# Feed-forward tail: modulation and residual folded into the accumulated rows ahead of the last products, sum of squares on ScalarE

## The reference, cut to what matters

```
def conv_glu(h, w_ffn_in, conv_w, conv_b, w_ffn_out):
    gate, val = jnp.split(h @ w_ffn_in, 2, axis=-1)            # D_FF = 2816 each
    gconv = conv_b + sum(gp[:, j:j + T] * conv_w[j] for j in range(CONV_W))
    return (jax.nn.gelu(gconv) * val) @ w_ffn_out

    x = x + gt1 * (mix @ lw['w_out'])                          # kept as x1
    h2 = rmsnorm(x, lw['g_ffn']) * (1.0 + sc2) + sh2
    x = x + gt2 * conv_glu(h2, ...)                            # gt2: a row of 1024, one per group
    ...
    y_prompt = rmsnorm(x_ctx, g_final)
    y_sample = rmsnorm(x_lat, g_final)
```

## Time and profile before

| what | value |
|---|---|
| runs | 2257.80, 2255.67, 2257.38 us; median 2257.38 us |
| profiled execution, its own time | 2254.62 us |
| its span, first to last instruction | 2252.8 us |
| mean granted TensorE clock | 0.971 |
| TensorE matmul busy | 2118.3 us (94%) |
| VectorE, ScalarE, GpSimd busy | 964.6 us (43%), 670.3 us (30%), 782.2 us (35%) |

### The profile page before, as it was taken

How to read it: one execution, slowest core, us unless ns; L and a number is a source line. 1 busy time by engine, 2 the same in 40 slices (tenths; PEclk the granted TensorE clock), 3 DMA queues, 4 the chain that set the end, 5 groups by cost and what they waited for, 6 DMA issues and landing times. The chain is left out here.

```text
span 2252.8 us, 28053 instructions
## 1 busy us (share of the span) xinstructions
PE 2118.3 (94%) x11544; PEld 1949.0 (87%) x11544; DVE 964.6 (43%) x1372; ACT 670.3 (30%) x954; POOL 782.2 (35%) x512
## 2 busy tenths in 40 slices
PE   7499999999999988999988789999999999999995
PEld 2489999999999977788878777999999999999994
DVE  2613434444313126556624438343344333433348
ACT  1334232323213242677753211311211121112120
POOL 0324252526113414445532522422332233223234
PEclk9699999999999989999999899999999999999998
DMA  6366111112121356233345331311111111111113
GB/s 236 112 214 83 38 52 31 53 31 66 59 72 44 96 149 180 62 95 105 93 112 153 129 120 66 94 47 38 47 39 47 38 48 47 38 38 47 48 66 131
DMA packets 189103, 183.88 MB, mean 82 GB/s; under 512 B 52743, under 2 KB 156896, under 8 KB 188976
## 3 DMA queue, kind: packets, MB, share of 16 engines
q1 hardware_dynamic: 187680, 177.37, 26.5%
q0 software_dynamic: 1296, 4.72, 0.6%
HBM read 141.32 MB, written 40.74 MB: 81 GB/s over the span
## 5 line engine op out<-in xcount | busy, mean ns | idle before, releaser
L129 POOL TENSOR_TENSOR s_w_lo<-s_w_raw,s_w_hi 128x1024 fp32r<-128x1024 f32 x86 | 219.9, 2558 | 509.0 <-ACT s_w_hi L124 509.0
L822 PE MATMUL s_psum<-h_hi,s_w_hi 128*128 128x384 f32 x1008 | 345.3, 346 | 26.1 <-POOL h_lo L250 26.1
L2525 PE MATMUL s_ps<-h_hi,s_w_hi 128*128 128x384 f32 x1056 | 353.3, 335 | 0.7 <-ACT gate_pad L2368 0.7
L2525 PE MATMUL s_ps<-h_hi,s_w_lo 128*128 128x384 f32 x1056 | 353.1, 334 | 0.0
L2525 PE MATMUL s_ps<-h_lo,s_w_hi 128*128 128x384 f32 x1056 | 353.1, 334 | 0.0
L822 PE MATMUL s_psum<-h_hi,s_w_lo 128*128 128x384 f32 x1008 | 337.9, 338 | 0.0
L822 PE MATMUL s_psum<-h_lo,s_w_hi 128*128 128x384 f32 x1008 | 337.9, 338 | 0.0
L822 PEld LDWEIGHTS s_psum<-h_hi,s_w_hi 128*128 128x128 f32 x1008 | 191.1, 190 | 36.1 <-issue 19.0
L2525 PEld LDWEIGHTS s_ps<-h_hi,s_w_hi 128*128 128x128 f32 x1056 | 198.3, 188 | 1.4 <-issue 1.0
L2525 PEld LDWEIGHTS s_ps<-h_lo,s_w_hi 128*128 128x128 f32 x1056 | 198.3, 188 | 0.4
L2525 PEld LDWEIGHTS s_ps<-h_hi,s_w_lo 128*128 128x128 f32 x1056 | 198.3, 188 | 0.0
(11 more groups left out here) (366 smaller groups left out, 3877.4 us busy)
## 6 DMA issues: line engine op xcount, KB each, us to landing
s_w_raw<-in_w_ffn_in SPq DMA_DIRECT2D x44, 512.0 KB, 3.7
s_w_raw<-in_w_in SPq DMA_DIRECT2D x41, 512.0 KB, 3.9
s_w_mod<-in_w_mod SPq DMA_DIRECT2D x8, 2048.0 KB, 8.0
w_raw<-in_w_ffn_out SPq DMA_DIRECT2D x11, 1024.0 KB
scratch_gates<-sig SPq DMA_DIRECT2D x48, 192.0 KB, 1.9
merge_gates<-scratch_gates SPq DMA_DIRECT2D x16, 576.0 KB, 4.4
w_mod<-in_w_mod SPq DMA_DIRECT2D x4, 2048.0 KB, 10.1
scratch_o_mla<-o_raw SPq DMA_DIRECT2D x8, 576.0 KB, 4.8
```

Of the source, the lines that this page charges most:

```text
L129: pool.tensor_tensor(flat[0], flat[1], flat[2], ALU.subtract).then_inc(self.lo_ready, 1)
L822: return pe.matmul(bank(j), wx[c % 2][:, k, :], hx[:, k, j * CH:(j + 1) * CH], start=(k == 0 and n == 0), stop=(k == KD - 1 and n == 2))
L2525: mm = pe.matmul(ps[bank][:, 0:CH], a[s][:, k, :], b[:, k, j * CH:(j + 1) * CH], start=n == 0, stop=n == 3 * KD - 1)
```

## The change

It does five things. (1) Ahead of the last products DVE multiplies each `yacc` tile by the `gt2` row (`z_gate`) and POOL adds the residual half by half (`z_add`), in the order tile 8 (the context), then 0 to 7. `z_gate(0)` stands in pair 9 after `y_add(8)`, `z_gate(1)` to `(4)` after the values of pair 9, `(5)` to `(8)` between the two convolutions of pair 10. On POOL `z_add(0)` and `(1)` stand ahead of `split_lo(42)`, `(2)` to `(4)` ahead of `split_lo(43)`, `(5)` and `(6)` ahead of `u_split(10, 0)`, `(7)` and `(8)` after `u_split(10, 1)`. (2) In the tail DVE multiplies the PSUM halves by the `gt2` row straight into `x2`, and POOL adds the `yacc` tile (DVE does it for the last tile). (3) The sum of squares is taken by ACT with an accumulating Square. (4) The residual is loaded in halves into a ring of four, the first four in pair 9 with a `gt2` row (`gt2_once`, loaded twice), the other 14 each after the `z_add` four halves before. (5) The convolution buffers start at a lower address. PE's stream is the same but for the semaphore of L2618.

```
         late = Arena(nc, after_h)
         yacc = late("yacc", [P, TILES, D])
-        over = Arena(nc, home.top)
+        over = Arena(nc, first.at)
...
+        gt2_once = over("gt2_once", [P, D])
+        x1_back = [over("x1_back3", [P, HALF])]
...
+        x1_back = [late(f"x1_back{i}", [P, HALF]) for i in range(3)] + x1_back
...
+        Z_TILES = (TILES - 1,) + tuple(range(TILES - 1))
...
+                def load_back(i):
+                    t, half = Z_TILES[i // 2], i % 2
+                    if i >= 4:
+                        sp.wait_ge(z_ready, i - 3)
+                    sp.dma_start(x1_back[i % 4][:, :], io["x1"][t * P:(t + 1) * P, half * HALF:(half + 1) * HALF]
+                                 ).then_inc(back_loaded[i % 4], 16)
...
                 for g in range(PAIRS):
+                    if g == LAST - 1:
+                        sp.dma_start(gt2_once[:, :], io["rows"][3:4, :].to_broadcast([P, D])).then_inc(once_loaded, 16)
+                        for i in range(4):
+                            load_back(i)
                     if g < LAST:
                         load_win(4 * g + 4)
                         load_win(4 * g + 5)
                         load_w2(g + 1)
+                    if g == LAST - 1:
+                        sp.wait_ge(z_gated, 1)
+                        sp.dma_start(gt2_once[:, :], io["rows"][2:3, :].to_broadcast([P, D])).then_inc(once_loaded, 16)
+                    if g < LAST:
                         load_win(4 * g + 6)
                         load_win(4 * g + 7)
+                for i in range(4, O_UNITS):
+                    load_back(i)
                 sp.wait_ge(v_ps, 6 * PAIRS)
...
                 for t in range(TILES):
-                    if t >= 3:
-                        sp.wait_ge(e_x2, t - 2)
-                    sp.dma_start(x1_back[t % 3][:, :], io["x1"][t * P:(t + 1) * P, :]).then_inc(back_loaded[t % 3], 16)
...
                     sp.wait_ge(e_fin, t + 1)
...
                 for t in range(TILES):
+                    act.wait_ge(e_x2, t + 1)
+                    if t >= 3:
+                        act.wait_ge(e_stored[t % 3], 16 * (t // 3))
+                    act.activation(fin[t % 3][:, :], x2[t % 3][:, :], ACT.Square, accum_out=stat[:, 3, t:t + 1]).then_inc(e_sq, 1)
                     act.wait_ge(e_sq, t + 1)
...
+                def z_add(n):
+                    pool.wait_ge(z_gated, n + 1)
+                    for i in (2 * n, 2 * n + 1):
+                        cols = slice(i % 2 * HALF, (i % 2 + 1) * HALF)
+                        pool.wait_ge(back_loaded[i % 4], 16 * (i // 4 + 1))
+                        z = yacc[:, Z_TILES[n], cols]
+                        pool.tensor_tensor(z, z, x1_back[i % 4][:, :], ALU.add).then_inc(z_ready, 1)
...
+                z_add(0)
+                z_add(1)
+                w.split_lo(pool, 0, 4 * LAST + 2)
+                for t in range(2, 5):
+                    z_add(t)
+                w.split_lo(pool, 1, 4 * LAST + 3)
+                z_add(5)
+                z_add(6)
+                u_split(LAST, 0)
+                w2_split(LAST)
+                u_split(LAST, 1)
+                z_add(7)
+                z_add(8)
+
+                pool.wait_ge(z_ready, O_UNITS)
+                for t in range(TILES - 1):
+                    pool.wait_ge(e_gated, 2 * t + 2)
+                    pool.tensor_tensor(x2[t % 3][:, :], x2[t % 3][:, :], yacc[:, t, :], ALU.add).then_inc(e_x2, 1)
...
-                        pe.wait_ge(e_sum, o - 7)
+                        pe.wait_ge(e_gated, o - 7)
...
+                def z_gate(n):
+                    t = Z_TILES[n]
+                    dve.wait_ge(once_loaded, 32 if n else 16)
+                    if n == 0:
+                        dve.wait_ge(y_added, O_UNITS * Y_PAIRS)
+                    dve.tensor_tensor(yacc[:, t, :], yacc[:, t, :], gt2_once[:, :], ALU.mult).then_inc(z_gated, 1)
+
                 for g in range(PAIRS):
                     conv_gate(g, 0)
                     if 0 < g < LAST:
                         y_add(g - 1)
+                    if g == LAST - 1:
+                        z_gate(0)
+                    if g == LAST:
+                        for n in range(5, TILES):
+                            z_gate(n)
                     conv_gate(g, 1)
                     value(g, 0)
                     value(g, 1)
...
+                    if g == LAST - 1:
+                        for n in range(1, 5):
+                            z_gate(n)
...
+                def end_gate(t):
+                    if t >= 3:
+                        dve.wait_ge(e_fin, t - 2)
                     for half in range(2):
                         o = 2 * t + half
+                        cols = slice(half * HALF, (half + 1) * HALF)
                         dve.wait_ge(e_ps, o + 1)
...
+                        dve.tensor_tensor(x2[t % 3][:, cols], ps[(6 + o) % 8][:, :], gt2[group(t)][:, cols], ALU.mult).then_inc(e_gated, 1)
...
                 for t in range(TILES):
-                    end_sums(t)
+                    end_gate(t)
+                    if t == TILES - 1:
+                        dve.wait_ge(e_gated, 2 * TILES)
+                        dve.wait_ge(z_ready, O_UNITS)
+                        dve.wait_ge(e_x2, TILES - 1)
+                        dve.tensor_tensor(x2[t % 3][:, :], x2[t % 3][:, :], yacc[:, t, :], ALU.add).then_inc(e_x2, 1)
                     if t >= 1:
-                        end_square(t - 1)
                         end_scale(t - 1)
-                end_square(TILES - 1)
                 end_scale(TILES - 1)
```

More of the change, by code:

```diff
@@ L2216, in stage_out_ffn @@
         w2_raw = over("w2_raw", [P, 2, D])
-        assert over.at <= HIGH
+        gt2_once = over("gt2_once", [P, D])
+        x1_back = [over("x1_back3", [P, HALF])]
+        assert over.at <= HIGH - 8
         w2_hi, w2_lo = late("w2_hi", [P, 2, D], F32R), late("w2_lo", [P, 2, D], F32R)
         u_hi, u_lo = late("u_hi", [P, 2, NT], F32R), late("u_lo", [P, 2, NT], F32R)
+        x1_back = [late(f"x1_back{i}", [P, HALF]) for i in range(3)] + x1_back
         assert late.at <= first_end
@@ L2235, in stage_out_ffn @@
         gfin = end("g_final_row", [P, D])
-        x1_back = [end(f"x1_back{i}", [P, D]) for i in range(3)]
         x2 = [end(f"x2_{i}", [P, D]) for i in range(3)]
@@ L2253, in stage_out_ffn @@
         y_ps, y_added = sems("y_product"), sems("y_added")
-        end_rows, back_loaded = sems("end_rows"), [sems(f"back_loaded{i}") for i in range(3)]
-        e_ps, e_sum, e_gated, e_x2 = sems("end_product"), sems("end_sum"), sems("end_gated"), sems("end_x2")
+        end_rows, once_loaded, back_loaded = sems("end_rows"), sems("once_loaded"), [sems(f"back_loaded{i}") for i in range(4)]
+        z_gated, z_ready = sems("z_gated"), sems("z_ready")
+        e_ps, e_gated, e_x2 = sems("end_product"), sems("end_gated"), sems("end_x2")
         e_sq, e_std, e_rstd = sems("end_sq"), sems("end_std"), sems("end_rstd")
@@ L2319, in _ @@
                     sp.dma_start(gt2[g][:, :], io["rows"][2 + g:3 + g, :].to_broadcast([P, D])).then_inc(end_rows, 16)
+                g_final = io["g_final"]
+                sp.dma_start(gfin[:, :], bass.AP(g_final.tensor, g_final.offset, [[0, P], [1, D]])).then_inc(end_rows, 16)
                 for t in range(TILES):
-                    if t >= 3:
-                        sp.wait_ge(e_x2, t - 2)
-                    sp.dma_start(x1_back[t % 3][:, :], io["x1"][t * P:(t + 1) * P, :]).then_inc(back_loaded[t % 3], 16)
[L2324 to L2331, removed]
                     sp.wait_ge(e_fin, t + 1)
@@ L2478, in _ @@
                 w.split_lo(pool, 0, 2)
-                for g in range(PAIRS):
+                def z_add(n):
[5 more added lines that the diff above has]
+                        pool.tensor_tensor(z, z, x1_back[i % 4][:, :], ALU.add).then_inc(z_ready, 1)
+                for g in range(LAST):
                     if g > 0:
@@ L2482, in _ @@
                     w.split_lo(pool, 1, 4 * g + 3)
-                    if g < LAST:
-                        w2_split(g)
+                    w2_split(g)
                     u_split(g, 0)
[L2486 to L2489, removed]
+                    w.split_lo(pool, 0, 4 * g + 4)
                     u_split(g, 1)
[L2491 to L2497, removed]
+                    w.split_lo(pool, 1, 4 * g + 5)
+                z_add(0)
[15 more added lines that the diff above has]
+                    pool.tensor_tensor(x2[t % 3][:, :], x2[t % 3][:, :], yacc[:, t, :], ALU.add).then_inc(e_x2, 1)
             @block.tensor
@@ L2721, in _ @@
                     value(g, 1)
-                def end_sums(t):
+                    if g == LAST - 1:
+                        for n in range(1, 5):
+                            z_gate(n)
+                dve.wait_ge(end_rows, 48)
+                def end_gate(t):
+                    if t >= 3:
+                        dve.wait_ge(e_fin, t - 2)
```

(8 more changed lines are left out.)

## The result

The first four runs of the changed kernel gave a median of 2237.19 us against 2256.98 before: ratio 0.9914, interval 0.9897 to 0.9931. That is faster, as forecast, but 0.8 under the low end of the range. With more runs on one chip (six against eleven) it was 2238.74 against 2256.38, ratio 0.9926, interval 0.9914 to 0.9938.

A forecast was written before the change was run, and what follows sets the result against it. VectorE was taken to bound the tail, 6.88 us a tile against TensorE's 5.53. The rearranged tail gave 15.8 less, TensorE's wait in pair 10 took back 1.0; 14.8 off the median 2257.38 gives 2242.6, range 2238 to 2249.

The forecast's parts named there:

- the sign that VectorE would wait for TensorE in every tile: Tail: VectorE's tile at 4.4 us, under TensorE's 5.53, so VectorE waits in every tile.
- That chain: Last tile, TensorE's end 2227.72 to scaling's end 2232.8: half product, add, square, root, reciprocal, scaling.
- The unseen price: Last tile's square on ScalarE: handing out the sum, between 0 and 0.3 us, taken as 0.1.
- Pair 10's locked work: VectorE and POOL in turn, from 2140.8 to the last convolution step: 24.7 us, so to 2165.5.
- the term of 1.0 for TensorE's wait in pair 10: Second value chunk in pair 10: TensorE waits 0.6 us, raised to 1.0 for lock turns and a late load.
- The store term of 0.3: Span's end: last two stores 1.6 us apart instead of 3, between 0 and 1.8 more, taken as 0.3.
- the 216 matmuls: Tail products: TensorE needs 49.8 us for all of them, 5.53 a tile.
- the low end: Whole time 2238: no wait (1.0 less), no store crowding (0.3), runs as low as the profiled one (2.8 below median).
- Rival 1: Pair 10: TensorE waits longer, from full locked work or a late half load, 4 to 10 us; around 2250, chance 0.12.
- Rival 2: Tail: a table load of 1.28 us between Square and root, perhaps doubled; 2244 to 2245, chance 0.08.
- Rival 3: Tail: VectorE or the lock still sets the pace, tile near 6.9 us; time near 2257, chance 0.04.
- Rival 4: Pair 10: late half loads hold POOL's in-order queue, TensorE stands 18 us or more; 2262 to 2270, chance 0.04.

The follow-up runs named there:

- experiments 2 and 3: Kernel before with only the sum of squares moved to ScalarE, ratio 0.9963; changed kernel with that sum back on VectorE, ratio 0.9955.
- no_z: Changed kernel without the moved gate multiplications, residual adds and their loads; from pair 10's first product to the span's end 133.2 us.
- after_again: Changed kernel run again without an edit; ratio 0.9926, from pair 10's first product to the span's end 133.35 us.
- extra1: Changed kernel plus one VectorE operation of 1,024 columns before pair 10's second convolution; from pair 10's first product to the span's end 137.1 us.
- extra2: Changed kernel plus two VectorE operations of 1,024 columns before pair 10's second convolution; from pair 10's first product to the span's end 140.3 us.

## Why the prediction was right and wrong

**Right, and shown.** The mechanism is the forecast's. TensorE never waited for VectorE before, and VectorE's tile of 6.9 against TensorE's 5.5 made the tail; with the tile under 5.5 the end is one tile's chain behind TensorE (experiments 2 and 3 put the tile at 6.0 and 5.67, and the last halves came 5.7 and 3.2 later than in the changed kernel). Not right was the sign that VectorE would wait for TensorE in every tile: it did from tile 4 on, and TensorE, which never waited for VectorE, lost nothing by it. That chain was worked out as 5.08 from TensorE's end to the last scaling's end, and took 2235.16 - 2230.16 = 5.0. The unseen price, handing out the sum on ScalarE, was taken as 0.1 within 0 to 0.3: it is 0.19. Pair 10's locked work was worked out to end 62.5 into the stage; it ended at 61.65. Half of the 0.85 is an earlier start (`z_add(0)` done 37.4 into the stage, not 37.8), half a shorter sum (24.3, not 24.7).

**Wrong by size, in the stage: 14.8 forecast, 16.4 measured.** The step that failed is the term of 1.0 for TensorE's wait in pair 10. The working gave 0.6, and I added to it for turns that cost something and a late load. Neither was there, and with the locked work ending 0.85 sooner the 0.6 was not there either: the wait is 0.09 (74.99 against 74.90), and no_z bounds all of the moved work at 0.2. Turns cost nothing beyond the operations' own lengths; residual halves landed in 2.4 to 7.5, each in time. The store term of 0.3 was 0.07 (3.94 from the last scaling's end to the span's end, against 3.87). And the 216 matmuls took 49.47 instead of 49.8, which I had held fixed, 0.3 more. These three and 0.1 of the last chain make up the 1.6; that all four went one way is luck.

**Wrong in the range.** The forecast time, 2242.6, lies 5.4 above the measured 2237.19. 1.6 of it is the stage, above; 0.4 is the median of before, which a fourth run moved; the rest, 3.4, isn't in the stage. I take it for scatter ahead of the stage, as after_again bears out: the same kernel at 2238.74, inside the range, with the same stage. Only one of the first four runs has a profile, so where in the other three it arose isn't shown. The failed step is the low end, which took its scatter, 2.8, from one execution of the kernel before against its own median and gave the changed kernel no more, and which had no room for a stage that comes out shorter by more than the wait and the store. The ten runs of the changed kernel so far lie between 2234.69 and 2244.48.

**The rivals.** Rival 1 (a longer wait in pair 10) didn't come, but extra1 and extra2 show it was close: 1.1 more of locked work cost 3.7, 2.2 cost 6.9. A distance of 0.4 us is luck. Its price, 4 to 10, fits these two only in size: I had priced the wait alone, and of the 6.9 the clock after it is 2.7. Rival 2 (table loads): the profile has one load in the tail, of 1.28, behind the first Square and off the chain:

```profile
2194.61 0.18 ACT L2450 ACTIVATION_READ_ACCUMULATOR final_rows<-x 128x1 f32 x1
2194.81 1.28 ACT L2452 ACT_TABLE_LOAD   x1
2196.11 0.29 ACT L2452 ACTIVATE s_stat<-s_stat,eps 128x1 f32<-128x1 f32 x1
2196.31 1.04 ACT L2450 ACTIVATE final_rows<-x 128x1024 f32<-128x1024 f32 x1
```

The next Square runs right behind a root with no load between, so the roots' table has Square in it. The root starts 1.30 after the load began. So this trace shows 1.3 for the switch and no drain after it, where the Trainium skill ("ScalarE: Activation LUTs", "What ACT_TABLE_LOAD costs") counts about 2.66. Rival 3: the tile didn't stay near 6.9, though the scaling nearly always waited, 3.45 and not the 2.77 that I had carried over; with it a tile's work is 4.75, still under 5.5. Rival 4 needed TensorE to stand for 18 us; the most that extra2 made it stand, by more work and not by a late load, was 4.3.

## What to carry to other kernels

Before pricing a tail by its busy engine, ask when TensorE finished. If it never waited, the tail is worth the difference of the two paces, summed over the tiles (12.1 here), and what leaves the last tile's own chain (4.4 here); once the other engine is under TensorE's pace, taking more work from it gains only in that last chain. In these traces VectorE operations with two SBUF inputs and GpSimd's take turns. Where both are full, an operation added on one costs its own length and can let in a turn of the other (2.4 later for 1.1 added, in extra1): count both engines' locked work in each stretch against every deadline of TensorE (here there were three, with 0.4, 2.1 and 1.0 to spare), and leave more than a turn (2.25 here) to spare. For effects below the scatter of the runs compare a stage between two events of the trace, not the medians.

## What was not expected of the hardware

- A wait of TensorE of 2.0 us (extra1) was followed by a stretch at 1.2 GHz that cost 1.8 more; one of 4.3 (extra2) by a longer one that cost 2.7. In the kernel before, a wait of 1.8 (until 885.23) was not followed by a fall.
- How soon the upper clock comes back after the same wait near 720 differs from run to run, and costs 0, 1.5 or 3 us there, in steps, with the same code. Part of it is made up later in the span.
- The turns of VectorE and GpSimd alternate strictly when both have work queued: the changed kernel's four multiplications of 1,024 columns take 9.02 with four half adds of 512 between them, 2.25 a pair, extra2's two further ones 4.43, and nothing is lost between turns.
- The one-tile TENSOR_SCALAR of the convolution, 0.88 in the earlier trace rows, took 1.85 beside POOL's adds in the changed kernel and 2.95 in extra2, so it waits too. VectorE's operations on a PSUM half kept 0.67 to 0.69 throughout.
